# Rotary half swap in the sliding attention layer by transfers inside SBUF in place of a permutation matmul

## The chip, the cores and the metric

The kernel runs on one core of one Trainium2 chip. The metric is the device time of one launch in microseconds (us). A core has a matrix engine (PE, TensorE), a vector engine (DVE), an activation engine (ACT), a general engine (POOL, GpSimd) and a sync engine (SP), each with an instruction stream of its own, and 16 DMA engines that move data between HBM and the on-chip memory SBUF, or inside SBUF. PSUM is the memory into which PE writes. Engines wait for one another through semaphores only. An engine runs its instructions in the order of its program: one that waits holds up all behind it.

## The reference

One inference step of a small encoder: 256 prompt frames and 32 sample frames, model width 1024. Layer 0 mixes by an mLSTM, layer 1 by sliding-window attention with 16 query heads, 4 key and value heads and width 64. Each mixer has half a SwiGLU feed-forward before and behind it. What the change touches is the rotary embedding of layer 1's queries and keys:

```python
def rope(x, pos):
    inv = ROPE_THETA ** (-jnp.arange(0, A_HD, 2, dtype=jnp.float32) / A_HD)
    ang = pos.astype(jnp.float32)[:, None] * inv[None, :]
    cos = jnp.cos(ang)[None, :, None, :]
    sin = jnp.sin(ang)[None, :, None, :]
    xf = x.astype(jnp.float32)
    x1, x2 = xf[..., : A_HD // 2], xf[..., A_HD // 2:]
    return jnp.concatenate([x1 * cos - x2 * sin, x2 * cos + x1 * sin], axis=-1).astype(x.dtype)

def swa_project(x, w_qkv, pos):
    ...
    q, k, v = jnp.split(x @ w_qkv, [A_HEADS * A_HD, (A_HEADS + A_KV_HEADS) * A_HD], axis=-1)
    q = rope(q.reshape(B, T, A_HEADS, A_HD), pos)
    k = rope(k.reshape(B, T, A_KV_HEADS, A_HD), pos)
```

Then come the scores with a mask and a sink, the softmax, the product with the values, and the output projection.

## The kernel before

Activations are kept with features on partitions: x is 8 chunks of 128 features by 288 tokens. Every weight product is made to nearly fp32 from three matmuls of rounded parts (hi*hi, hi*lo, lo*hi; `products`, L360 to L362), so one **piece** (128 output features, 8 input chunks) is 24 matmuls of 288 columns on PE. The weights stream from HBM: SP issues one transfer of 1 MB for two pieces (L303) into one of two `raw` buffers, ACT rounds a piece to `whi` (L340, `split_hi`), DVE subtracts to get `wlo` (L347, `split_lo`), and PE multiplies. SP may load unit u when both pieces of unit u-2 have been subtracted (`lo_done`, L322).

The program is twelve stages, one behind the other. Stage 8, `swa_in`, makes the 12 pieces of the attention layer in the order of `SWA_PIECES`: k0, q0, v0, q1, q2, q3, k1, q4, q5, q6, v1, q7. Numbers 0 to 11 of this list are called **steps** below, step n being what an engine does around piece n. `lo_ahead` in step n subtracts the weights of piece n+4; step 1 does it for pieces 4 and 5.

Rotary: DVE copies a q or k piece out of PSUM to `s_raw` (L1201). PE multiplies it by a permutation matrix `perm`, which exchanges the 32-partition halves of each head (L642, an fp32 product of 288 columns into a PSUM bank of the ring `acc`). DVE multiplies the result by sin into `s_t2` (L1219). POOL makes the product with cos (`s_t1`, L1332) and the sum (L1336), which is the rotated piece. `ROPE` is the list of the ten pieces that are not v.

The attention itself is cut into 20 items (16 of prompt, 4 of sample) that run as a pipeline of **ticks** between the pieces: from step 4 on there are two ticks in a step. In tick t PE makes scores of items t and t+1 if t is even (L578, L580, L585), transposes the probabilities of item t-2 (L595 to L598), and multiplies by the values (L614, L621, L625); DVE takes mask and row maximum of item t's scores (L1149, L1152, `scores`) and divides item t-1 (L1163 to L1167, `divide`); ACT does the exponentials (L867), copies out the transposed probabilities (L852) and the results (L842). Scores of item t on PE need the rotated q (`rope_done`) and the maximum of item t-1 (`neg_ready`). v pieces are transposed on PE (L646, "turn") and copied by DVE (L1223, L1224).

The order of the groups of PE and DVE around this is the list `SWA_GROUPS`, 24 entries: 12 pieces, 10 swaps, each behind the next piece, and 2 turns. The ticks hang on entries of this list (`SWA_TICKS`). Ticks 16 to 23 (`TAIL_TICKS`) follow step 11 and are mixed with parts of stage 9, `mix_out`.

Of the kernel before, what the change touches and what calls it, by code (L numbers as in the profile page):

```python
# [43 lines left out]
          ("swa_in", 6, 24, 8), ("mix_out", 4, 8, 8), ("ffn_in", 22, 44, 8), ("ffn_out", 8, 8, 11)]  # L44
# [15 lines left out]
for _n, _p in enumerate(SWA_PIECES):  # L60
    SWA_GROUPS.append(("piece", _p))
    if _n and SWA_PIECES[_n - 1] in ROPE:
        SWA_GROUPS.append(("swap", SWA_PIECES[_n - 1]))
    if _p in TURN_AFTER:
        SWA_GROUPS.append(("turn", TURN_AFTER[_p]))
SWA_GROUPS.append(("swap", SWA_PIECES[-1]))
# [8 lines left out]
SWA_TICKS = {}  # L75
for _n in range(FIRST_TICK, len(SWA_PIECES)):
    _g = SWA_GROUPS.index(("piece", SWA_PIECES[_n]))
    SWA_TICKS[SWA_GROUPS[_g]], SWA_TICKS[SWA_GROUPS[_g + 1]] = 2 * (_n - FIRST_TICK), 2 * (_n - FIRST_TICK) + 1
TAIL_TICKS = range(2 * (len(SWA_PIECES) - FIRST_TICK), len(ITEMS) + 4)

# [16 lines left out]
C_ID, C_ONE, C_PERM, C_TRI, C_SEL = 0, 128, 256, 384, 640  # L97
# [7 lines left out]
def constants():  # L105
# [5 lines left out]
    c[p, C_PERM + (p ^ 32)] = 1.0  # L111
# [18 lines left out]
def program(nc, a):  # L130

    ctx = ExitStack()
    with ctx:
# [21 lines left out]
        cst = sb("cst", [P, 3 * P])  # L155
# [9 lines left out]
        ident, ones, perm = cst[:, 0:P], cst[:, P:2 * P], cst[:, 2 * P:3 * P]  # L165
# [35 lines left out]
        s_qs = w(9920, 2, 4 * TS)  # L201

# [70 lines left out]
        t1_ready = sem("t1_ready")  # L273
        rope_done = sem("rope_done")
# [24 lines left out]
        def _(sp):  # L299
# [75 lines left out]
        def _(pe):  # L375
# [17 lines left out]
            def in_piece(i, it, c, g, G):  # L393
# [4 lines left out]
                products(pe, group_bank(g), c % 4, [(k, k) for k in range(KD)], xhi, xlo, True, True).then_inc(piece_done, 1)  # L398
# [168 lines left out]
            def tick(t, G0):  # L567
# [32 lines left out]
                if t >= 4 and t % 2 == 0:  # L600
# [3 lines left out]
                    pe.wait_ge(evac, G0 + group_of("turn", f"v{c // 4 if kind == 'p' else c}") + 1)  # L604
# [23 lines left out]
            def swa_in(i):  # L628
                c0_, G0 = 2 * FIRST_UNIT[i], FIRST_GROUP[i]
                pe.wait_ge(mix_in, MIX_SWA)  # L630
                for g, (what, p) in enumerate(SWA_GROUPS):
                    n = SWA_PIECES.index(p)
                    bank = group_bank(g)
                    if what == "piece":
                        if n == 0:
                            first_two(i, c0_, G0)
                        if n > 1:
                            in_piece(i, 0, c0_ + n, g, G0 + g)
                    elif what == "swap":
# [3 lines left out]
                    else:  # L643
                        pe.wait_ge(evac, max(G0 + group_of("piece", p) + 1, G0 + g - 3))
                        for t, (at, m) in enumerate(TOK):
                            mm = pe.transpose(acc[(g + BANK) % 4][0:m, t * P:(t + 1) * P], s_vT[:, at:at + m], ident)  # L646
                        mm.then_inc(turn_mm, 1)
                    if (what, p) in SWA_TICKS:
                        tick(SWA_TICKS[what, p], G0)

# [35 lines left out]
        def _(act):  # L686
# [183 lines left out]
            def swa_in(i, norm):  # L870
# [4 lines left out]
                for what, p in SWA_GROUPS:  # L875
                    if what == "piece":
                        hi_ahead(0, c0_ + SWA_PIECES.index(p))
                    if (what, p) in SWA_TICKS:
                        tick(SWA_TICKS[what, p])
# [7 lines left out]
            for m in range(KD):  # L887
                if m == 4:
                    act.dma_start(cst[:, :], a["cst"][:, 0:3 * P]).then_inc(cst_in, 16)
# [40 lines left out]
        def _(dve):  # L930
# [257 lines left out]
            def swa_in(i, norm):  # L1188
                c0_ = 2 * FIRST_UNIT[i]
                for g, (what, p) in enumerate(SWA_GROUPS):  # L1190
                    n = SWA_PIECES.index(p)
                    bank = group_bank(g)
                    xi = ROPE.index(p) if p in ROPE else None
                    if what == "piece":
                        dve.wait_ge(piece_done, c0_ + n + 1)
                        if xi is None:
                            dve.tensor_tensor(s_vT[:, :], bank, rstd[:, :], ALU.mult).then_inc(evac, 1)
                        else:
                            if xi >= 2:
                                dve.wait_ge(t1_ready, xi - 1)  # L1200
                            dve.tensor_copy(s_raw[:, xi % 2, :], bank).then_inc(evac, 1)  # L1201
                        if n == 1:
# [4 lines left out]
                            own(dve.tensor_tensor(rs, sin, rstd[:, :], ALU.mult))  # L1207
                        if n >= FIRST_TICK:
                            divide(2 * (n - FIRST_TICK))
                        if n == 1:  # L1210
                            lo_ahead(0, c0_)
                        if n > 0:
                            lo_ahead(0, c0_ + n)
                    else:
                        dve.wait_ge(turn_mm, TURNS.index((what, p)) + 1)
                        if what == "swap":
                            if xi >= 2:
                                dve.wait_ge(rope_done, xi - 1)
                            dve.tensor_tensor(s_t2[:, xi % 2, :], bank, rs, ALU.mult).then_inc(evac, 1)  # L1219
                        else:  # L1220
                            j = int(p[1]) * P
                            bank = acc[(g + BANK) % 4]
                            dve.tensor_copy(s_v[0:TS, 2, j:j + P], bank[0:TS, 2 * P:3 * P])  # L1223
                            dve.tensor_copy(s_v[:, 0:2, j:j + P], bank[:, 0:2 * P].rearrange("p (t c) -> p t c", t=2))\  # L1224
                                .then_inc(evac, 1)
                    if (what, p) in SWA_TICKS:
# [219 lines left out]
```

## Time and profile before

| what | us |
|---|---|
| time, median of 3 runs | 1119.02 |
| lowest and highest run | 1117.14, 1119.58 |
| span of the profiled execution (first to last instruction) | 1116.9 |
| PE busy | 1099.2 (98%) |
| DVE busy | 707.9 (63%) |
| ACT busy | 510.8 (46%) |
| POOL busy | 126.0 (11%) |

The profiled execution has no time of its own in the records beside its span of 1116.9 us; the span is 2.1 us under the median of the runs. "Busy" is an average over all twelve stages; the attention stage (about 802 to 875 us) has other shares than the rest, so it is read from windows of its own. In a row of the trace a start is in us from the span's start, and L642 is line 642 of the kernel.

### The profile page before, as it was taken

The numbers are of one execution on the slowest core, as the hardware profiler recorded it, in microseconds if no ns is written. First come the engines' busy times: TensorE is split into PE (matmuls) and PEld (weight loads), VectorE is DVE, ScalarE is ACT, GpSimd is POOL, SyncE is SP. The second block draws the span as 40 slices with busy tenths as digits, with TensorE's granted clock in tenths as the row PEclk, the third lists the DMA queues.
The fourth block names the chain that finished last, engine by engine and source line by source line (L and its number), as shares of the span: only waits on it lengthen the run. The fifth ranks groups of instructions, "written<-read, shape, count | busy, mean of one in ns | idle before, by whom it ended". The sixth has DMA issues, their size and how long they took to land.

```text
span 1116.9 us, 21215 instructions
## 1 busy us (share of the span) xinstructions
PE 1099.2 (98%) x8113; PEld 1075.8 (96%) x8113; DVE 707.9 (63%) x1073; ACT 510.8 (46%) x760; POOL 126.0 (11%) x159
## 2 busy tenths in 40 slices
PE   8999999999999999999999999999999999999996
PEld 7999999998999999999999999999988899999996
DVE  7766665564665866666546666645599776666442
ACT  6444443354454544444335444433466554444331
POOL 3000001100002600000120000011142410000011
PEclk9999999999999999999999999999999999999998
DMA  6544454432332654445434544543332244444531
GB/s 235 188 172 166 153 204 156 151 107 102 127 123 89 216 188 150 172 180 184 179 113 154 182 153 156 204 176 141 113 142 97 82 172 162 173 165 178 182 129 43
DMA packets 24203, 172.04 MB, mean 154 GB/s; under 512 B 3248, under 2 KB 3536, under 8 KB 5600
## 3 DMA queue, kind: packets, MB, share of 16 engines
q1 hardware_dynamic: 21888, 167.16, 41.6%
q0 software_dynamic: 960, 2.23, 0.6%
q10 hardware_dynamic: 1312, 2.07, 0.5%
q8 instruction: 29, 0.48, 0.2%
q14 instruction: 14, 0.11, 0.0%
HBM read 168.88 MB, written 2.56 MB: 153 GB/s over the span
## 4 chain that ended last, share of the span: by engine, by line
PE 93%; DVE 3%; ACT 2%; DMA 1%; issue 1%; POOL 0%; DVEq 0%; ACTq 0%; SPq 0%
PE acc L360 30%; PE acc L362 29%; PE acc L361 29%; DVE wlo L347 1%; DMA raw<-in_w 1%; DVE rstd L946 1%; PE mb L595 0%; ACT whi L340 0%; PE mb L614 0%; PE mb L529 0%; PE num L521 0%; PE acc L642 0%; ACT work L867 0%; PE mb L387 0%; PE num L524 0%
## 5 line engine op out<-in xcount | busy, mean ns | idle before, releaser
L360 PE MATMUL acc<-xhi,whi 128*128 128x288 f32 x1696 | 508.1, 300 | 3.3 <-DVE xlo L941 2.8
L340 ACT ACTIVATE whi<-raw 128x1024 fp32r<-128x1024 f32 (+1 forms) x292 | 328.8, 1128 | 390.1 <-PE acc L362 373.7
L361 PE MATMUL acc<-xlo,whi 128*128 128x288 f32 x1696 | 502.3, 296 | 0.0
L362 PE MATMUL acc<-xhi,wlo 128*128 128x288 f32 x1696 | 500.5, 295 | 0.0
L347 DVE TENSOR_TENSOR wlo<-raw,whi 128x1024 fp32r<-128x1024 f32 (+1 forms) x292 | 389.2, 1333 | 158.7 <-ACT whi L340 148.7
L360 PEld LDWEIGHTS acc<-xhi,whi 128*128 128x128 f32 x1696 | 319.6, 188 | 7.2 <-issue 4.5
L362 PEld LDWEIGHTS acc<-xhi,wlo 128*128 128x128 f32 x1696 | 321.3, 189 | 0.0
L361 PEld LDWEIGHTS acc<-xlo,whi 128*128 128x128 f32 x1696 | 320.4, 189 | 0.5
L360 PE MATMUL acc<-ahi,whi 128*128 128x288 f32 x832 | 247.1, 297 | 0.9 <-DVE alo L1179 0.7
L361 PE MATMUL acc<-alo,whi 128*128 128x288 f32 x832 | 245.4, 295 | 0.0
L362 PE MATMUL acc<-ahi,wlo 128*128 128x288 f32 x832 | 244.6, 294 | 0.0
L360 PEld LDWEIGHTS acc<-ahi,whi 128*128 128x128 f32 x832 | 155.9, 187 | 2.2 <-issue 1.2
L362 PEld LDWEIGHTS acc<-ahi,wlo 128*128 128x128 f32 x832 | 156.7, 188 | 0.0
L361 PEld LDWEIGHTS acc<-alo,whi 128*128 128x128 f32 x832 | 156.2, 188 | 0.0
L968 DVE TENSOR_TENSOR work<-acc,rstd 128x288 f32<-128x288 f32 x88 | 40.2, 456 | 59.5 <-PE acc L362 58.7
L1280 POOL TENSOR_TENSOR ssq<-x 128x288 f32<-128x288 f32 x7 | 4.7, 665 | 612.3 <-DVE x L995 582.9
L1291 POOL TENSOR_TENSOR sqr<-x 128x288 f32<-128x288 f32 x44 | 42.6, 969 | 201.9 <-DVE x L995 197.8
L964 DVE TENSOR_TENSOR work<-acc,rstd 128x288 f32<-128x288 f32 x88 | 40.2, 456 | 34.8 <-PE acc L362 34.6
L745 ACT ACTIVATE xhi<-x,norms (+1 forms) x24 | 12.9, 537 | 92.4 <-DVE x L995 92.4
L995 DVE SCALAR_TENSOR_TENSOR x<-acc,x 128x288 f32 (+1 forms) x32 | 14.6, 458 | 61.2 <-PE acc L362 61.2
L971 DVE TENSOR_TENSOR work<-work 128x288 f32<-128x288 f32 x88 | 40.3, 458 | 6.9 <-DVE work L968 2.2
L719 ACT ACTIVATE ahi<-work 128x288 f32 (+1 forms) x88 | 39.0, 443 | 10.8 <-DVE work L971 8.7
(208 smaller groups left out, 618.4 us busy)
## 6 DMA issues: line engine op xcount, KB each, us to landing
raw<-in_w SPq DMA_DIRECT2D x113, 1024.0 KB, 4.8
raw<-in_w SPq DMA_DIRECT2D x32, 1408.0 KB, 5.8
x<-in_xT SPq DMA_DIRECT2D x4, 288.0 KB, 5.8
raw<-in_w SPq DMA_DIRECT2D x2, 512.0 KB, 5.2
out_yT<-x ACTq DMA_DIRECT2D x3, 288.0 KB, 2.3
work<-in_cst POOLq DMA_DIRECT2D x1, 560.0 KB, 4.0
work<-in_c ACTq DMA_DIRECT2D x1, 514.0 KB
out_cp<-work POOLq DMA_DIRECT2D x4, 128.5 KB, 2.4
```

The source lines that it names most:

```text
L340: act.activation(dst, src, ACT.Copy).then_inc(hi_done, 1)
L347: dve.tensor_tensor(dst, src, hi, ALU.subtract).then_inc(lo_done, 1)
L360: pe.matmul(out, wh, hi[:, k, :], start=(first and n == 0), stop=False)
L361: pe.matmul(out, wh, lo[:, k, :], start=False, stop=False)
L362: mm = pe.matmul(out, wl, hi[:, k, :], start=False, stop=(last and n == len(tiles) - 1))
L719: act.activation(ahi[:, bass.ds(2 * it + u, 1), :], f_prod[:, u % 2:u % 2 + 1, :], ACT.Copy)\
L745: act.activation(xhi[:, m, :] if norm < N_FINAL else xg[:, m, :], x[:, m, :], ACT.Copy, scale=norms[:, norm, m]).then_inc(xhi_done, 1)
L964: dve.tensor_tensor(f_gate[:, b, :], group_bank(2 * u), rstd[:, :], ALU.mult).then_inc(evac, 1)
L968: dve.tensor_tensor(f_up[:, b, :], group_bank(2 * u + 1), rstd[:, :], ALU.mult).then_inc(evac, 1)
L971: dve.tensor_tensor(f_prod[:, b, :], f_silu[:, b, :], f_up[:, b, :], ALU.mult).then_inc(prod_done, 1)
L995: dve.scalar_tensor_tensor(x[:, m, :], acc[u][:, 0:T].rearrange("p (a t) -> p a t", a=1), 0.5, x[:, m, :], ALU.mult, ALU.add).then_inc(eva ...
L1291: pool.tensor_tensor(sqr[:, m % 2, :], x[:, m, :], x[:, m, :], ALU.mult).then_inc(pool_sq, 1)
```

## The change

The permutation matmul and its matrix are dropped. A piece's half swap is made by four transfers inside SBUF, of 32 partitions each, from `s_raw` to a new buffer `s_swap`, issued by SP (`halves_swapped`); SP's loads for stages 8 and 9 are written out by hand so that the swaps can stand among them. DVE's product with sin reads `s_swap` (`swapped`), directly behind the `lo_ahead` of the next step and ahead of both ticks. `SWA_GROUPS` has 16 entries: 12 pieces, 2 turns, and 2 "last" (the third transpose of a turn, now a group of its own). On PE the odd tick stands in the middle of a piece (`between`).

```diff
-STAGES: ("swa_in", 6, 24, 8)
+STAGES: ("swa_in", 6, 16, 8)
...
+            def swa_load(u):
+                i, m = (8, u) if u < STAGES[8][1] else (9, u - STAGES[8][1])
+                sp.wait_ge(lo_done, 2 * (FIRST_UNIT[8] + u - 2) + 2)
+                load(a[f"w{i}"][m], 8, 0, FIRST_UNIT[8] + u)
+
+            def halves_swapped(xi, p):
+                b = xi % 2
+                sp.wait_ge(evac, FIRST_GROUP[8] + group_of("piece", p) + 1)
+                if xi >= 2:
+                    sp.wait_ge(t2_ready, xi - 1)
+                for at in range(0, P, 32):
+                    sp.dma_start(s_swap[at:at + 32, b, :], s_raw[at ^ 32:(at ^ 32) + 32, b, :]).then_inc(swap_in[b], 16)
...
+                if i == 8:
+                    for u in range(4):
+                        swa_load(u)
+                    for n, p in enumerate(SWA_PIECES):
+                        if n % 2 == 0:
+                            swa_load(4 + n // 2)
+                        if p in ROPE:
+                            halves_swapped(ROPE.index(p), p)
+                if i in (8, 9):
+                    continue
...
 PE, swa_in
-                        pe.wait_ge(evac, max(G0 + group_of("piece", p) + 1, G0 + g - 3))
-                        pe.matmul(bank, perm, s_raw[:, ROPE.index(p) % 2, :], start=True, stop=True).then_inc(turn_mm, 1)
...
+                            t = 2 * (n - FIRST_TICK) - 1
+                            in_piece(i, 0, c0_ + n, g, G0 + g, between=(lambda: tick(t, G0)) if t > 0 else None)
+                        if p in SWA_TICKS:
+                            tick(SWA_TICKS[p], G0)
...
 DVE, swa_in
+                def swapped(xi):
+                    b = xi % 2
+                    dve.wait_ge(swap_in[b], SWAP * (xi // 2 + 1))
+                    if xi >= 2:
+                        dve.wait_ge(rope_done, xi - 1)
+                    dve.tensor_tensor(s_t2[:, b, :], s_swap[:, b, :], rs, ALU.mult).then_inc(t2_ready, 1)
...
                         if n > 0:
                             lo_ahead(0, c0_ + n)
+                        if n and SWA_PIECES[n - 1] in ROPE:
+                            swapped(ROPE.index(SWA_PIECES[n - 1]))
+                        if p in SWA_TICKS:
+                            tick(SWA_TICKS[p])
+                            tick(SWA_TICKS[p] + 1)
...
-                            dve.tensor_tensor(s_t2[:, xi % 2, :], bank, rs, ALU.mult).then_inc(evac, 1)
...
+                swapped(len(ROPE) - 1)
                 for t in TAIL_TICKS:
...
 POOL
-                pool.wait_ge(evac, G0 + group_of("swap", p) + 1)
+                pool.wait_ge(t2_ready, xi + 1)
```

SP's queue in stages 8 and 9. Before, it holds loads only (`w8` and `w9` are the weights of stages 8 and 9; each waits for `lo_done`):

```order
L303 ISA [waits lo_done]
L303 DMA raw<-in_w8 128x2048
L322 REGISTER_ALU
L303 ISA [waits lo_done]
L303 DMA raw<-in_w8 128x2048
```

Now, from the first load of stage 8 (units 0 to 4) to the swaps of steps 4 and 5:

```order
L302 DMA raw<-in_w8 128x2048 [waits lo_done] x5
L324 DMA work<-work 32x288 [waits evac]
L324 DMA work<-work 32x288 x3
L324 DMA work<-work 32x288 [waits evac]
L324 DMA work<-work 32x288 x3
L302 DMA raw<-in_w8 128x2048 [waits lo_done]
L324 DMA work<-work 32x288 [waits t2_ready,evac]
L324 DMA work<-work 32x288 x3
L302 DMA raw<-in_w9 128x2048 [waits lo_done]
L324 DMA work<-work 32x288 [waits t2_ready,evac]
L324 DMA work<-work 32x288 x3
L324 DMA work<-work 32x288 [waits t2_ready,evac]
```

The swap of an even step stands behind a load that waits for `lo_done`; the swap of the odd step behind it follows at once.

DVE in steps 1 to 3, before (L347 is the subtraction, L1219 the product with sin, L1197 and L1201 the evacuations of a piece):

```order
L347 TENSOR_TENSOR wlo<-raw,whi 128x1024 [waits hi_done,vector_chain]
L347 TENSOR_TENSOR wlo<-raw,whi 128x1024 [waits hi_done]
L1219 TENSOR_TENSOR work<-acc0,work 128x288 [waits turn_mm]
L1197 TENSOR_TENSOR work<-acc1,rstd 128x288 [waits piece_done]
L347 TENSOR_TENSOR wlo<-raw,whi 128x1024 [waits hi_done]
L1219 TENSOR_TENSOR work<-acc2,work 128x288 [waits turn_mm]
L1201 COPY work<-acc3 128x288 [waits t1_ready,piece_done]
```

And now (L370, L1225, L1233, L1238 are the same operations):

```order
L370 TENSOR_TENSOR wlo<-raw,whi 128x1024 [waits hi_done,vector_chain]
L370 TENSOR_TENSOR wlo<-raw,whi 128x1024 [waits hi_done]
L1225 TENSOR_TENSOR work<-work 128x288 [waits swap_in0]
L1233 TENSOR_TENSOR work<-acc0,rstd 128x288 [waits piece_done]
L370 TENSOR_TENSOR wlo<-raw,whi 128x1024 [waits hi_done]
L1225 TENSOR_TENSOR work<-work 128x288 [waits swap_in1]
L1238 COPY work<-acc1 128x288 [waits t1_ready,piece_done]
```

The wait of the product with sin has moved from a matmul of PE (`turn_mm`) to the landing of the transfers (`swap_in0`, `swap_in1`); its place behind the subtractions is the same here. From step 5 on it stands ahead of both ticks' maxima in place of between them:

```order
L370 TENSOR_TENSOR wlo<-raw,whi 128x1024 [waits hi_done]
L1225 TENSOR_TENSOR work<-work 128x288 [waits rope_done,swap_in1]
L1177 ISA work<-num,work 128x128 [waits s_mm]
L1177 ISA work 128x1
L1177 ISA work<-num,work 128x256
```

## Rows read from the trace of the kernel before

**Rows 1.** The page: span and busy time of the engines.

```profile
span 1116.9 us, 21215 instructions
...
PE 1099.2 (98%) x8113; PEld 1075.8 (96%) x8113; DVE 707.9 (63%) x1073; ACT 510.8 (46%) x760; POOL 126.0 (11%) x159
```

**Rows 2.** Window: length, busy PE, PEld, DVE, ACT, POOL, granted clock, DMA share, GB/s.

```profile
815.00:860.00 45.00, 44.60 (x354) 37.46 (x355) 42.77 (x155) 28.39 (x95) 12.51 (x21) 1.00 0.25 93
```

**Rows 3.** Chain in order of time, one step of PE: start us, us, what.

```profile
824.79 0.42 PE num L578 x4
825.21 0.43 PE num L580 x4
...
826.95 0.68 PE acc L642 x2
...
831.15 0.42 PE num L578 x4
```

**Rows 4.** Timeline of DVE, step 6: start, us, line, tiles.

```profile
825.46 0.45 DVE L1201 COPY work<-acc 128x288 f32<-128x288 f32 x1
...
828.62 0.45 DVE L1219 TENSOR_TENSOR work<-acc,work 128x288 f32<-128x288 f32 x1
...
831.60 0.44 DVE L1201 COPY work<-acc 128x288 f32<-128x288 f32 x1
```

**Rows 5.** Timeline of DVE, subtractions and marks of steps 1 to 5.

```profile
806.20 2.85 DVE L347 TENSOR_TENSOR wlo<-raw,whi 128x1024 fp32r<-128x1024 f32 x2
...
812.04 1.26 DVE L347 TENSOR_TENSOR wlo<-raw,whi 128x1024 fp32r<-128x1024 f32 x1
...
816.23 0.28 DVE L1149 CUSTOM_DVE_ANT_0 work<-num,work 128x128 f32<-128x128 f32 x1
...
820.88 1.22 DVE L347 TENSOR_TENSOR wlo<-raw,whi 128x1024 fp32r<-128x1024 f32 x1
```

**Rows 6.** Timeline of SP: starts of loads 4 and 6 of stage 8.

```profile
809.22 0.33 SPq L303 DMA_DIRECT2D raw<-in_w  x1
...
822.27 0.33 SPq L303 DMA_DIRECT2D raw<-in_w  x1
```

**Rows 7.** Issues: tiles, queue, count, KB, median us to landing; load 4, then the page.

```profile
raw<-in_w SPq DMA_DIRECT2D x1, 1024.0 KB, 4.8
...
out_yT<-x SPq DMA_DIRECT2D x1, 288.0 KB, 2.3
```

**Rows 8.** Timeline of SP at the program's start, transfers issued behind one another.

```profile
2.14 0.43 SPq L311 DMA_DIRECT2D raw<-in_w  x1
2.62 1.02 SPq L312 DMA_DIRECT2D x<-in_xT  x2
```

**Rows 9.** Issues of those two starts, alone: KB, us to landing.

```profile
raw<-in_w SPq DMA_DIRECT2D x1, 512.0 KB, 6.1
...
x<-in_xT SPq DMA_DIRECT2D x1, 288.0 KB, 6.4
```

**Rows 10.** Timeline of POOL: sum and product with cos; DVE's division beside it, then alone.

```profile
829.15 0.81 POOL L1336 TENSOR_TENSOR work<-work 128x288 f32<-128x288 f32 x1 [3.95 <-DVE work L1219]
...
830.19 0.81 POOL L1332 TENSOR_TENSOR work<-work 128x288 f32<-128x288 f32 x1
...
830.35 0.99 DVE L1167 TENSOR_SCALAR work<-work 128x128 f32<-128x128 f32 x2
...
832.34 0.55 DVE L1167 TENSOR_SCALAR work<-work 128x128 f32<-128x128 f32 x2
```

**Rows 11.** Timeline of DVE: subtraction of step 11 and maximum of tick 16.

```profile
857.79 1.21 DVE L347 TENSOR_TENSOR wlo<-raw,whi 128x1024 fp32r<-128x1024 f32 x1
...
863.62 0.28 DVE L1149 CUSTOM_DVE_ANT_0 work<-num,work 128x128 f32<-128x128 f32 x1
```

**Rows 12.** Windows at the span's end, columns as in rows 2.

```profile
1108.00:1110.00 2.00, 0.00 (x0) 0.00 (x0) 1.48 (x1) 0.49 (x1) 0.00 (x0) 0.96 0.01 4
1110.00:1112.00 2.00, 0.00 (x0) 0.00 (x0) 1.97 (x4) 0.00 (x0) 1.45 (x2) 0.50 0.00 0
```

More of the change, by code:

```diff
@@ L59 @@
 SWA_GROUPS = []
-for _n, _p in enumerate(SWA_PIECES):
+for _p in SWA_PIECES:
     SWA_GROUPS.append(("piece", _p))
-    if _n and SWA_PIECES[_n - 1] in ROPE:
-        SWA_GROUPS.append(("swap", SWA_PIECES[_n - 1]))
     if _p in TURN_AFTER:
-        SWA_GROUPS.append(("turn", TURN_AFTER[_p]))
-SWA_GROUPS.append(("swap", SWA_PIECES[-1]))
+        SWA_GROUPS += [("turn", TURN_AFTER[_p]), ("last", TURN_AFTER[_p])]
 TURNS = [g for g in SWA_GROUPS if g[0] != "piece"]
@@ L74 @@
 FIRST_TICK = 4
[L75 to L78, printed above, removed]
+SWA_TICKS = {_p: 2 * (_n - FIRST_TICK) for _n, _p in enumerate(SWA_PIECES) if _n >= FIRST_TICK}
 TAIL_TICKS = range(2 * (len(SWA_PIECES) - FIRST_TICK), len(ITEMS) + 4)
+SWAP = 64
 FILL = {}
@@ L94 @@
 N_F1, N_FINAL, N_HEAD = 0, 6, 7
[L97 removed]
+C_ID, C_ONE, C_TRI, C_SEL = 0, 128, 256, 512
 C_COS = C_SEL + NH * P
@@ L164, in program @@
         work = sb("work", [P, 12496])
-        ident, ones, perm = cst[:, 0:P], cst[:, P:2 * P], cst[:, 2 * P:3 * P]
+        ident, ones = cst[:, 0:P], cst[:, P:2 * P]
         def w(at, *shape):
@@ L391, in ss_sum, with in_piece @@
                 mm.then_inc(ss_mm, 1)
-            def in_piece(i, it, c, g, G):
+            def in_piece(i, it, c, g, G, between=None):
                 pe.wait_ge(lo_done, 4 * it + c + 1)
@@ L397, in in_piece @@
                     pe.wait_ge(evac, 4 * it + G - 3)
-                products(pe, group_bank(g), c % 4, [(k, k) for k in range(KD)], xhi, xlo, True, True).then_inc(piece_done, 1)
+                if between is None:
+                    products(pe, group_bank(g), c % 4, [(k, k) for k in range(KD)], xhi, xlo, True, True).then_inc(piece_done, 1)
+                    return
+                products(pe, group_bank(g), c % 4, [(k, k) for k in range(KD // 2)], xhi, xlo, True, False)
+                between()
+                products(pe, group_bank(g), c % 4, [(k, k) for k in range(KD // 2, KD)], xhi, xlo, False, True)\
+                    .then_inc(piece_done, 1)
             def first_two(i, c, G):
@@ L603, in tick @@
                     pe.wait_ge(pt_ready, t - 2)
-                    pe.wait_ge(evac, G0 + group_of("turn", f"v{c // 4 if kind == 'p' else c}") + 1)
+                    pe.wait_ge(evac, G0 + group_of("last", f"v{c // 4 if kind == 'p' else c}") + 1)
                     if t >= 6:
@@ L637, in swa_in @@
                         if n > 1:
[L638 to L645 removed]
+                            t = 2 * (n - FIRST_TICK) - 1
+                            in_piece(i, 0, c0_ + n, g, G0 + g, between=(lambda: tick(t, G0)) if t > 0 else None)
+                        if p in SWA_TICKS:
+                            tick(SWA_TICKS[p], G0)
+                        continue
+                    pe.wait_ge(evac, max(G0 + group_of("piece", p) + 1, G0 + g - 3))
+                    for t, (at, m) in enumerate(TOK):
+                        if (t == 2) == (what == "last"):
                             mm = pe.transpose(acc[(g + BANK) % 4][0:m, t * P:(t + 1) * P], s_vT[:, at:at + m], ident)
[L647 to L649 removed]
+                    mm.then_inc(turn_mm, 1)
+                tick(TAIL_TICKS[0] - 1, G0)
             def swa_out(i):
@@ L874, in swa_in @@
                 act.activation(warm[:, 9:10], epst[:, :], ACT.Exp)
[L875 to L879, printed above, removed]
+                for n, p in enumerate(SWA_PIECES):
+                    hi_ahead(0, c0_ + n)
+                    if p in SWA_TICKS:
+                        tick(SWA_TICKS[p])
+                        tick(SWA_TICKS[p] + 1)
                 for t in TAIL_TICKS:
@@ L1341, in _ @@
             pool.dma_start(a["kT_out"], s_k[:, :, TP - P:T]).then_inc(out_dma, 16)
-            pool.wait_ge(evac, G0 + group_of("turn", "v1") + 1)
+            pool.wait_ge(evac, G0 + group_of("last", "v1") + 1)
             pool.dma_start(a["v_out"][0:P, :], s_v[:, 1, :]).then_inc(out_dma, 16)
```

35 lines of the change are left out of this document (17 added, 18 removed).

## The prediction

> **What bounds the kernel now.** The page comes first: of a span of 1116.9 us PE is busy for 1099.2 and DVE for 707.9 [rows 1]. Over the whole program PE is the bound, and work taken from PE looks like time won. But the change lies in one stage, so the second view is the window of that stage alone: from 815 to 860 us, steps 4 to 11, PE is busy for 44.60 of 45.00 us and DVE for 42.77, which is 95% [rows 2]. There are two bounds here, and the less loaded one is hardly idle. The third view is the stage in order of time. On PE one step repeats from 824.79 to 831.15, 6.36 us, and holds one permutation of 0.68 us [rows 3]. On DVE the same step runs from one evacuation at 825.46 to the next at 831.60, 6.14 us [rows 4]. The fourth view is SP's queue, which the change puts to a new use: load 4 starts at 809.22, when the two subtractions of step 1 end (806.20 + 2.85 = 809.05), and load 6 at 822.27, when that of step 5 ends (820.88 + 1.22 = 822.10) [rows 5, 6]. So in an odd step n SP's load starts 0.17 us behind DVE's `lo_ahead(n)`; by the code this holds for steps 1, 3, 5, 7, 9 and 11.
>
> **What is removed.** Ten permutations of 0.68 us [rows 3], 6.8 us of PE. The most that this can bring is 6.8 us, if PE alone set the end. It does not: with 0.68 taken away PE's step is 5.68 us and DVE's stays 6.14, since DVE's own work is the same list of operations (the product with sin only reads SBUF in place of PSUM; no row prices that form, and I leave it at the 0.45 us of L1219 [rows 4], some 0.4 from start to start). Even with a free swap a step falls from 6.36 to 6.14 only. The matrix's smaller constant load and the eight groups fewer in `SWA_GROUPS` cost nothing and win nothing: the banks of PSUM are freed by the evacuations as before. The odd tick in the middle of a piece keeps PE supplied while it waits for a transpose's input; PE will not be the bound, so I put it at nothing.
>
> **What is added, and where it waits.** Forty transfers of 36 KB. Their place in SP's queue decides. Take step 5. DVE ends `lo_ahead(5)` and then, as its next instruction, wants the swapped q2. SP meanwhile holds load 6 at the head of its queue, which waits for exactly that `lo_ahead(5)`; q2's four transfers are queued behind it. So although q2 was in `s_raw` a whole step earlier, its swap is only issued when DVE is already asking for it, and the whole flight of the transfer is a wait of DVE. The same meets k0 in step 1, k1 in step 7 and q5 in step 9. The swaps of the odd pieces (q0, q3, q4, q6) follow directly behind the even ones and are asked for a step later, so they are hidden. q1 and q7 are odd pieces that stand behind a load of their own (v0 and v1 need no swap), and are counted apart below.
>
> **The price of one such wait, W.** From the end of `lo_ahead(n)`: 0.17 us until the load starts, then the load's own flight of 4.8 us [rows 7], if transfers of one queue are served in their order, then the swaps' own share. The program's start shows the order: a 512 KB transfer issued at 2.14 lands 6.1 later, at 8.24; one of 288 KB issued right behind it at 2.62 lands 6.4 later, at 9.02 [rows 8, 9]. The later one lands later, by 0.8 us for 288 KB. Four swaps are 144 KB, so half of that, 0.4. W = 0.17 + 4.8 + 0.4 = 5.4 us. Lower end: the swaps pass the load. Then SP's issues count: the load's 0.33, three swaps of about 0.5 before the last [rows 6, 8], and a flight of 2.3 us, which is the 288 KB output alone on its queue [rows 7]: 0.17 + 0.33 + 1.5 + 2.3 = 4.3. Upper end: each transfer touches 32 partitions where the 288 KB one touches 128; if it is four times as slow for that, 1.6 in place of 0.4: W = 6.6. I take 5.4, since its rows show this very queue in this very situation.
>
> A rule of the notes bears on W. The Trainium skill, DMA: Bandwidth & Descriptors, section "Anatomy of one DMA", gives about 2.0 us of fixed cost for each transfer plus its bytes at 436 GB/s. By it load and swaps together (1.2 MB) would take an estimated 4.7 us, W would be 4.9, and the time some 3 us less than by the rows. The section "Queues, rings and completion order" of the same page has descriptors taken up in ring order, and with that the landings of rows 8 and 9 agree.
>
> **What is queued behind the wait.** On DVE: both ticks' row maxima and the division, then the next evacuation. ACT's exponentials wait for the maxima, and PE's next scores (even tick) wait for `neg_ready` from them. PE can still do its even tick, the next piece and the odd tick's transposes, and then stands. Nothing on DVE can be drawn ahead, so W is paid in full.
>
> **The sum,** as the shift of DVE's work against its times of before.
> - Step 1: k0's swap arrives at 809.05 + 5.4 = 814.45. Then two products with sin, two evacuations (0.4 each) and two subtractions (1.2 each [rows 5]), 4.0 in all: `lo_ahead(3)` ends at 818.45. Before it ended at 812.04 + 1.26 = 813.30 [rows 5].
> - Step 4: load 5 starts then, and q1's swap lands 5.4 later, at 823.85. The turn's copies, q2's evacuation and `lo_ahead(4)` fill 2.2 of it. First maximum at 824.25, before 816.23 [rows 5]: +8.0, and +7.6 at the start of step 5, as the product with sin is already done.
> - Steps 5, 7, 9: 3 x 5.4 = +16.2, in all +23.8.
> - Back: DVE's division takes 0.99 us while POOL runs L1332 beside it, and 0.55 alone [rows 10]. Now POOL's sum and product start 0.8 us earlier in the tick and are mostly over by then: 8 odd ticks x 0.44 = 3.5 at most. DVE's few idle gaps (45.00 - 42.77 = 2.2) are partly filled too. I take 3.0: +20.8.
> - Tail: q7's swap is issued behind load 9, which waits for `lo_ahead(11)`. From the end of that subtraction (859.00 [rows 11]) the first maximum of tick 16 comes after W 5.4, the product 0.4, POOL's start and sum 0.15 + 0.81 [rows 10], PE's start and scores 0.1 + 0.85 [rows 3]: 7.7. Before it came at 863.62, 4.6 later [rows 11]. +3.1: +23.9.
> - PE's clock. In each of the long waits PE stands: of a pair of steps of some 17 us it has 2 x 5.68 = 11.4 us of work, so about 5.5 us in one piece. The trace shows what a stop does: with no matmul after 1108 the granted clock is 0.96 from 1108 to 1110 and 0.50, 1.2 in place of 2.4 GHz, from 1110 on [rows 12]. So part of the work behind each stop runs at half rate. Most of it lies under DVE; not so in the tail, where tick by tick PE is in the chain. Below 0 this cannot be. Above: PE takes up work again when W's end is 2.0 us past (product and two maxima), and has a whole step, 5.7, before the next piece is finished, at 7.7; DVE asks for that piece at 3.7 + 6.1 = 9.8. At half rate the step costs 5.7 more, of which 2.1 fit there: 3.6 a pair, 11 for three. I take 2, nearer to nothing, because the stops are short against the work between them and DVE has the later work. +26.
>
> The Trainium skill, TensorE: Matmul & The Clock Gate, section "What's actually happening", says the same of an idle array (1.2 GHz when cold, 2.4 when busy); rows 12 agree.
>
> 1119.0 + 26 = **1145 us**. The sum was made on the profiled execution, whose span is 2.1 us under the median; the shift is added to the median.
>
> **The rivals.**
> (a) The swap is hidden, the kernel is faster. That holds if a swap lands before DVE asks, by an SP that isn't held behind `lo_done`, or a landing within a fraction of a us. Then steps 5 to 11 gain 0.2 each, the two permutations ahead of step 4 bring 1.4: about 3 us, 1116. Against it stand rows 5 and 6 and the order of SP's queue. Chance 4%.
> (b) The swaps pass the load. W = 4.3: six waits (steps 1, 4, 5, 7, 9, tail) of 1.1 less, and no clock lost: 23.9 - 6.6 = 17, 1136. For it: nothing shows how transfers inside SBUF stand to one from HBM. Chance 18%.
> (c) Slow 32-partition transfers, or the half clock in the path: W = 6.6 adds 6 x 1.2 = 7, the clock takes 11 in place of 2: 23.9 + 7 + 11 = 42, 1161. Decided by how much of PE's work behind a stop runs at 1.2 GHz. Chance 20% for the half of this way and beyond.
> (d) The change doesn't do what it says, because the wait only takes the place of one that was there: then the time is within 0.2% of before, which is about what a measurement of this kernel can tell from no change. DVE at 95% speaks against it. 1%.
>
> **How the numbers follow.** Forecast 57%, 1139 to 1151, time 1145. (b) 18%, (c) 20%, (a) 4%, (d) 1%. The range 1135 to 1160 takes in (b) and (c) and leaves out (a), (d) and the edges. Faster by over 0.2%: 4%. Within: 1%. Slower: 95%.
>
> **What the profile of the changed kernel would show.** DVE idle ahead of the product with sin, released by the swap's transfer, in steps 1, 4, 5, 7, 9 and behind tick 15, about 5 us in four of them, and next to none in steps 2, 6, 8 and 10. SP's swaps of even steps starting right behind a load, and landing behind it. The window of steps 4 to 11 about 20 us longer, PE's busy share in it down to some 70%, with dips of the granted clock. Division at 0.55 in place of 0.99. All other stages alike. I would be wrong if DVE's waits are near 2 us or absent (then the queue isn't served as I say), or if the waits are there and the span is longer by much less (then DVE wasn't the bound), or by much more (then PE at half rate is).

## The result, and the profile after

The changed kernel takes 1161.1 us (median) against 1119.3 before: a ratio of 1.0367, with a 95% interval of 1.0343 to 1.0392. The forecast was 1145, in a range of 1135 to 1160. It is slower, as forecast, by the mechanism that was forecast, but by 42 us and not by 26, and the time lies a little outside the range. Of its four executions one took 3743.66 us, stands apart as slow and is left out of the ratio; the other three lie between 1156.25 and 1161.21.

The page of the changed kernel, answering to rows 1:

```profile
span 1159.3 us, 21181 instructions
...
PE 1110.0 (96%) x8093; PEld 1085.3 (94%) x8093; DVE 707.6 (61%) x1073; ACT 510.9 (44%) x760; POOL 126.1 (11%) x159
```

DVE's busy time has not changed (707.9 before), though the span is 42.4 us longer. PE has twenty instructions fewer (the ten permutations, each of two passes) and is busy for 10.8 us more: part of its work ran slower.

Windows of the attention stage (length, busy PE, PEld, DVE, ACT, POOL, granted clock, DMA share, GB/s). Before, 815 to 860 us was 99% PE and 95% DVE at a clock of 1.00 [rows 2]. After:

```profile
815.00:835.00 20.00, 13.01 (x82) 11.81 (x83) 11.85 (x31) 4.62 (x13) 7.18 (x9) 0.83 0.32 115
835.00:855.00 20.00, 13.22 (x98) 10.84 (x97) 11.84 (x44) 8.49 (x27) 3.54 (x6) 0.83 0.22 68
855.00:875.00 20.00, 14.74 (x105) 12.55 (x103) 10.82 (x38) 7.74 (x25) 3.52 (x6) 0.83 0.23 72
875.00:895.00 20.00, 14.74 (x99) 11.96 (x97) 12.98 (x51) 8.56 (x29) 3.57 (x6) 0.74 0.18 64
```

DVE is idle for 35 to 46% of each window and PE for 26 to 35%. Step 5 shows where the idle time comes from. The timelines of DVE and SP (L370 is the subtraction, L1225 the product with sin; L302 loads, L324 swaps; in brackets the idle time ahead of an instruction and what ended it):

```profile
834.14 1.22 DVE L370 TENSOR_TENSOR wlo<-raw,whi 128x1024 fp32r<-128x1024 f32 x1
841.46 0.46 DVE L1225 TENSOR_TENSOR work<-work 128x288 f32<-128x288 f32 x1 [6.10 <-DMA work<-work]
...
835.38 0.33 SPq L302 DMA_DIRECT2D raw<-in_w  x1
835.82 4.94 SPq L324 DMA_DIRECT2D work<-work  x8
```

The subtraction ends at 835.36, SP's load starts at 835.38, q2's four swaps from 835.82, and DVE stands for 6.10 us. SP's order is what was read from its queue; each issue of a swap takes 0.6 us. Who DVE and PE waited for in the whole stage (us in total, times, longest):

```profile
DVE work L1225 <- DMA work<-work: 28.4, 6, 6.1
DVE work L1238 <- PE acc L385: 7.4, 5, 2.7
DVE work L1191 <- ACT work L896: 6.0, 12, 2.6
...
PE num L607 <- DVE work L1180: 14.1, 3, 6.8
PE acc L675 <- DVE work L1233: 6.9, 1, 6.9
PE num L607 <- POOL work L1373: 6.2, 1, 6.2
```

Exactly six waits for the swaps, as counted: 6.1 us in steps 1, 5, 7 and 9 (6.11, 6.10, 5.95, 6.04), 1.4 in step 4, 2.8 in the tail.

To compare kernels, the stage is measured from the start of load 3 on SP to the first output of stage 9 on DVE. Before, from 799.44, 77.45 us; after, 116.32:

```profile
799.44 0.33 SPq L303 DMA_DIRECT2D raw<-in_w  x1
...
876.89 0.46 DVE L1014 TENSOR_TENSOR x<-acc,x 128x288 f32<-128x288 f32 x1 [1.95 <-PE acc L362]
```

```profile
803.00 10.11 SPq L302 DMA_DIRECT2D raw<-in_w  x2
...
919.32 0.46 DVE L1042 TENSOR_TENSOR x<-acc,x 128x288 f32<-128x288 f32 x1 [1.95 <-PE acc L385]
```

That is 38.9 us. The other 3.5 us of the two spans' difference lie ahead of the stage, in the mLSTM stage, which the change does not touch. There PE's clock falls for some us in nearly every kernel, for a length that differs; the profile of the changed kernel caught a long one. The same window of before and of after:

```profile
245.00:270.00 25.00, 24.85 (x150) 21.57 (x149) 16.68 (x42) 11.75 (x27) 0.00 (x0) 0.93 0.37 126
```

```profile
245.00:270.00 25.00, 24.85 (x134) 21.88 (x133) 15.60 (x42) 11.16 (x25) 0.00 (x0) 0.80 0.28 91
```

PE does not stop there. In the changed kernel the fall comes while it works on products of four rows, with no gap above 0.15 us; the window from 251 to 253 is at 0.53, where 0.50 is 1.2 GHz:

```profile
249.16 1.21 PE L514 MATMUL mb<-work 4*128 4x288 f32 x4
250.22 0.64 PE L514 MATMUL num<-work 4*128 4x288 f32 x2
251.01 1.24 PE L514 MATMUL num<-work 4*128 4x288 f32 x2 [0.15 <-DVE acol L1072]
```

```profile
251.00:253.00 2.00, 1.99 (x5) 1.23 (x6) 2.00 (x10) 1.38 (x5) 0.00 (x0) 0.53 0.94 393
```

In the kernel before, the clock stays at 1.00 behind the same products and falls behind the next group of four rows, some 6 us later; in e6 below it stays at 1.00 behind both.

In the profiles of the other kernels this stage's clock in the window from 245 to 270 lies between 0.80 and 1.00, and load 3 starts between 796.15 and 803.00, the later the lower that clock, with up to 2 us between kernels of the same clock. So a total time below carries some 3 us of chance from a stage that is the same everywhere, and the length of the attention stage is the sharper measure.

### The profile page after: what moved, and what is told of

It is laid out like the page before. It is cut to its first block, busy times and chain, and to the rows that moved or that the text cites. A ratio compares the mean times of both kernels' runs of the same rounds, so it can differ in the third digit from the quotient of the medians.

```text
span 1159.3 us, 21181 instructions
## 1 busy us (share of the span) xinstructions
PE 1110.0 (96%) x8093; PEld 1085.3 (94%) x8093; DVE 707.6 (61%) x1073; ACT 510.9 (44%) x760; POOL 126.1 (11%) x159
## 4 chain that ended last, share of the span: by engine, by line
PE 90%; DVE 4%; DMA 2%; ACT 1%; SPq 1%; issue 1%; DVEq 0%; POOL 0%; ACTq 0%
PE acc L383 29%; PE acc L384 28%; PE acc L385 28%; DMA work<-work 2%; DVE wlo L370 1%; SPq L324 1%; PE mb L643 1%; PE mb L624 1%; DVE rstd L974 1%; DMA raw<-in_w 0%; ACT whi L363 0%; PE mb L558 0%; PE num L550 0%; DVE work L1177 0%; PE num L609 0%
## 5 line engine op out<-in xcount | busy, mean ns | idle before, releaser
L370 DVE TENSOR_TENSOR wlo<-raw,whi 128x1024 fp32r<-128x1024 f32 (+1 forms) x292 | 388.9, 1332 | 161.2 <-ACT whi L363 151.3
L383 PEld LDWEIGHTS acc<-xhi,whi 128*128 128x128 f32 x1696 | 323.2, 191 | 8.8 <-issue 6.5
L385 PEld LDWEIGHTS acc<-xhi,wlo 128*128 128x128 f32 x1696 | 325.0, 192 | 0.0
L384 PEld LDWEIGHTS acc<-xlo,whi 128*128 128x128 f32 x1696 | 324.1, 191 | 0.3
L773 ACT ACTIVATE xhi<-x,norms (+1 forms) x24 | 12.9, 537 | 92.4 <-DVE x L1023 92.4
```

The costliest lines, as they stand in the source:

```text
L370: dve.tensor_tensor(dst, src, hi, ALU.subtract).then_inc(lo_done, 1)
L383: pe.matmul(out, wh, hi[:, k, :], start=(first and n == 0), stop=False)
L384: pe.matmul(out, wh, lo[:, k, :], start=False, stop=False)
L385: mm = pe.matmul(out, wl, hi[:, k, :], start=False, stop=(last and n == len(tiles) - 1))
L773: act.activation(xhi[:, m, :] if norm < N_FINAL else xg[:, m, :], x[:, m, :], ACT.Copy, scale=norms[:, norm, m]).then_inc(xhi_done, 1)
```

## The experiments

All kernels on one table. "q7" is the time from load 3 to the evacuation of q7, the "tail" the rest of the stage; both from the one profiled execution.

| kernel | time, us | ratio to before (95%) | stage | q7 | tail |
|---|---|---|---|---|---|
| before | 1118.7 to 1119.3 | 1 | 77.45 | 56.74 | 20.71 |
| changed | 1161.1 | 1.0367 (1.0343, 1.0392) | 116.32 | 88.50 | 27.82 |
| e1 swap first | 1123.2 | 1.0030 (1.0015, 1.0045) | 81.86 | 57.45 | 24.41 |
| e2 load behind | 1146.3 | 1.0235 (1.0209, 1.0261) | 105.67 | 78.22 | 27.45 |
| e3 PE busy in steps | 1156.3 | 1.0329 (1.0304, 1.0355) | 115.61 | 87.54 | 28.07 |
| e4 no transfers | 1123.4 | 1.0042 (1.0025, 1.0059) | 81.86 | 57.46 | 24.40 |
| e5 q7's product early | 1121.9 | 1.0026 (1.0010, 1.0041) | 79.24 | 57.43 | 21.81 |
| e6 products between ticks | 1119.4 | 1.0012 (0.9997, 1.0027) | 79.76 | 55.89 | 23.87 |
| e7 one transfer | 1155.0 | 1.0334 (1.0311, 1.0357) | 114.68 | 87.19 | 27.49 |
| e8 PE busy in steps and tail | 1153.5 | 1.0302 (1.0275, 1.0329) | 111.82 | 85.96 | 25.86 |
| e9 before, no permutation | 1117.7 | 0.9996 (0.9985, 1.0007) | 76.42 | 55.76 | 20.66 |
| e10 q7 by permutation | 1117.7 | 0.9990 (0.9975, 1.0004) | 76.54 | 55.86 | 20.68 |

**Theory and rival.** The theory was that the loss is the place of the swaps in SP's queue, behind a load that itself waits for DVE. The rival was that the transfers are slow or disturb the stage wherever they stand.

### e1: the swaps ahead of the load

```diff
                     for n, p in enumerate(SWA_PIECES):
-                        if n % 2 == 0:
-                            swa_load(4 + n // 2)
                         if p in ROPE:
                             halves_swapped(ROPE.index(p), p)
+                        if n % 2 == 1:
+                            swa_load(4 + n // 2)
```

> The changed kernel with SP's queue in another order: the swaps of an even and an odd step stand ahead of the load that waits for lo_ahead, not behind it; nothing else differs. Theory (the swaps are late only because they queue behind a load that waits for DVE): a swap is issued when its piece is evacuated, lands some 4.5 us later, before DVE asks for it; the six waits of 28.4 us in all are gone, and the time is 1113 to 1119. Rival (transfers inside SBUF of 32 partitions are slow or disturb the stage wherever they stand): waits of over 3 us remain and the time stays over 1135.

The stage falls from 116.32 to 81.86 us, and DVE no longer waits for a single swap. The rival is refuted: the forty transfers as such cost the stage nothing. But the time is 1123.2, above the 1119 expected and clearly above before. The theory holds for 34.5 of the 38.9 us; 4.4 are something else.

### e4: no transfers at all

```diff
...
-                    dve.wait_ge(swap_in[b], SWAP * (xi // 2 + 1))
+                    dve.wait_ge(evac, FIRST_GROUP[8] + group_of("piece", ROPE[xi]) + 1)
...
-                    dve.tensor_tensor(s_t2[:, b, :], s_swap[:, b, :], rs, ALU.mult).then_inc(t2_ready, 1)
+                    dve.tensor_tensor(s_t2[:, b, :], s_raw[:, b, :], rs, ALU.mult).then_inc(t2_ready, 1)
```

SP issues loads only, so the product reads the unswapped piece.

> The changed kernel without the 40 transfers; the product with sin reads the unswapped piece, so the rotary embedding is wrong and the time is that of a swap that costs nothing. Theory (DVE is the second bound of the stage): not the 6.8 us of the permutations but about 3 come back, 1115 to 1117. Rival (PE was the only bound): 1112.

Both expectations miss: with a swap that costs nothing the new order is slower than before, 1.0042, with a stage of 81.86 us, equal to e1's. So the 4.4 us are not the transfers' either. Its profile names two causes. First, PE stands for q7. Who PE waited for:

```profile
PE num L604 <- POOL work L1371: 4.3, 2, 3.7
```

q7's product stands behind both last ticks on DVE (`swapped` after the loop), so POOL's sum comes late, PE stands 3.7 us ahead of tick 16, and the granted clock over 855 to 875 is 0.91. Second, DVE's step has not become shorter. The end of step 7 in the kernel before, where the step took 6.13 us (831.60 [rows 4] to 837.73):

```profile
836.09 0.17 DVE L1163 TENSOR_TENSOR work<-work 128x2 f32<-128x2 f32 x1
...
836.49 0.99 DVE L1167 TENSOR_SCALAR work<-work 128x128 f32<-128x128 f32 x2
...
837.73 0.44 DVE L1201 COPY work<-acc 128x288 f32<-128x288 f32 x1
```

And step 7 in e4:

```profile
832.32 0.45 DVE L1236 COPY work<-acc 128x288 f32<-128x288 f32 x1
...
836.45 0.29 DVE L1174 CUSTOM_DVE_ANT_0 work<-num,work 128x128 f32<-128x128 f32 x1 [0.16 <-issue]
...
837.53 0.16 DVE L1188 TENSOR_TENSOR work<-work 128x2 f32<-128x2 f32 x1 [0.17 <-ACT work L893]
...
837.92 0.55 DVE L1192 TENSOR_SCALAR work<-work 128x128 f32<-128x128 f32 x2
...
838.72 0.45 DVE L1236 COPY work<-acc 128x288 f32<-128x288 f32 x1
```

It takes 6.40. The division is down to 0.55 us from 0.99 [rows 10], as forecast. But with the product no longer between the two maxima, DVE waits 0.16 us ahead of the second maximum and 0.17 us for ACT's exponentials ahead of the division, where before it waited for neither, and smaller gaps open between its own dependent instructions.

### e9: the kernel before without permutations

```diff
-                        pe.wait_ge(evac, max(G0 + group_of("piece", p) + 1, G0 + g - 3))
-                        pe.matmul(bank, perm, s_raw[:, ROPE.index(p) % 2, :], start=True, stop=True).then_inc(turn_mm, 1)
...
-                            dve.tensor_tensor(s_t2[:, xi % 2, :], bank, rs, ALU.mult).then_inc(evac, 1)
+                            dve.tensor_tensor(s_t2[:, xi % 2, :], s_raw[:, xi % 2, :], rs, ALU.mult).then_inc(evac, 1)
```

> The kernel before without the ten permutations on PE; the product with sin reads the unswapped piece (the rotary embedding is wrong), all else in the old order. Prices what the change takes away. If DVE is the second bound: 1115 to 1117. If PE alone was the bound: 1112.

The stage shortens by 1.0 us of the 6.8 that the permutations occupy on PE, less than the 2 to 4 expected, and the ratio cannot be told from 1. With DVE's work in this order that is all there was to win: DVE is the second bound, right behind PE.

### e2: the wait kept, the load behind

```diff
-                            swa_load(4 + n // 2)
+                            sp.wait_ge(lo_done, 2 * (FIRST_UNIT[8] + 4 + n // 2 - 2) + 2)
                         if p in ROPE:
                             halves_swapped(ROPE.index(p), p)
+                        if n % 2 == 1:
+                            swa_load(4 + n // 2)
```

> The changed kernel, but only the load is moved behind the swaps of its pair of steps; SP still waits for lo_ahead before the even swap. Tells what of the 6.1 us wait is the load in front. If the load's flight sets the landing: the wait falls to 0.2 + 4 issues of 0.6 + a flight of about 2 us = 4.3 to 4.6, six times 1.5 less, time about 1150. If SP's issues and the swaps' own flight set it: the wait falls by the load's issue of 0.44 only, to 5.7, time about 1158.

The long waits fall from 6.1 to 3.8 us, below even the 4.3 to 4.6 expected for a load that sets the landing. The issues of four swaps, just behind the subtraction, in this kernel and behind a load in the changed one (KB each, us to landing):

```profile
work<-work SPq DMA_DIRECT2D x4, 36.0 KB, 1.9
```

```profile
raw<-in_w SPq DMA_DIRECT2D x1, 1024.0 KB, 5.3
work<-work SPq DMA_DIRECT2D x4, 36.0 KB, 4.3
```

A swap alone lands in 1.9 us, behind a load in 4.3. So of the 6.1 us, 2.3 are the load in front, and 3.8 are a transfer's own flight with three issues ahead of the last. The stage is 10.7 us shorter (six waits of up to 2.3 us less; 9 expected); the time fell by 14.8; in the profiles 3.5 of that lie ahead of the stage, where load 3 starts at 799.54.

### e7: one transfer in place of four

```diff
-SWAP = 64
+SWAP = 16
...
-                for at in range(0, P, 32):
-                    sp.dma_start(s_swap[at:at + 32, b, :], s_raw[at ^ 32:(at ^ 32) + 32, b, :]).then_inc(swap_in[b], 16)
+                sp.dma_start(s_swap[:, b, :], s_raw[:, b, :]).then_inc(swap_in[b], 16)
```

> The changed kernel with one transfer of all 128 partitions for a piece in place of four of 32, in the same place of SP's queue; it swaps nothing, so the rotary embedding is wrong. Tells what of the 6.1 us is four issues of 0.6 us. If SP's issues make the landing late: 0.17 + 0.43 + a flight of 4 to 4.5 = 4.8 to 5.1, time about 1155 (six waits of 1 us less). If the load in front sets it: 5.6 to 6.0, time 1159 to 1161.

It swaps nothing. The longest wait is 5.9 us and the sum of the six 26.8, against 6.1 and 28.4; the stage is 1.6 us shorter. Behind a load the number of issues hardly matters: the queue is what sets the landing. The time of 1155.0 looks like the other answer, but 4.2 us of the difference between the two profiles lie ahead of the stage (load 3 starts at 798.84, in the changed kernel at 803.00); the stage decides.

### e3 and e8: PE kept busy while it waits

`keep_busy` and the fillers of steps 6, 8 and 10 are in both; the 44 at q1, ahead of v0's turn, are in e3 alone, the 40 ahead of tick 16 in e8 alone.

```diff
+            def keep_busy(g, G0, count):
+                pe.wait_ge(evac, G0 + g - 2)
+                for _ in range(count):
+                    pe.matmul(group_bank(g + 1), xhi[:, 0, 0:P], xhi[:, 0, :], start=True, stop=True)
...
+                        if n in (6, 8, 10):
+                            keep_busy(g, G0, 40)
...
+                        if p == "q1":
+                            keep_busy(g, G0, 44)
...
+                    if t == TAIL_TICKS[0]:
+                        pe.wait_ge(evac, FIRST_GROUP[i])
+                        for _ in range(40):
+                            pe.matmul(group_bank(3), xhi[:, 0, 0:P], xhi[:, 0, :], start=True, stop=True)
```

> The changed kernel with matmuls of no use in PE's stops: 40 before the even tick of steps 6, 8 and 10 and 44 before the turn of v0 (about 5.3 and 5.9 us), written to the next free bank. DVE's waits for the swaps stay at 6 us. Theory (the rest of the miss is work at 1.2 GHz behind the stops): the granted clock stays 1.00 there, DVE's waits for PE (1.3 us in steps 9 and 11, 1.75 in step 4) vanish, time 1148 to 1154. Rival (DVE's waits alone make the loss, the clock is covered): 1159 to 1162, or later if the fillers overrun the stops.

> The changed kernel with 40 matmuls of no use ahead of the even tick of steps 6, 8 and 10, as in the run before with fillers, but none at v0's turn and 40 ahead of tick 16, where PE stands 6 us for q7. Tells how much of the tail's loss (from q7's evacuation to the first output of the next stage 27.8 us, 20.7 before) is work at 1.2 GHz. If the clock is the larger part of what the wait for q7 doesn't explain: the tail falls to 25.5 or less. If it is covered: 27.5 to 28.5.

First the rows on the clock in the changed kernel. PE stops at about 837 in step 5 and takes up work at 843.9:

```profile
835.00:840.00 5.00, 2.11 (x17) 1.88 (x15) 0.36 (x1) 0.00 (x0) 0.00 (x0) 1.00 0.71 228
840.00:845.00 5.00, 1.11 (x8) 0.94 (x8) 3.19 (x16) 2.15 (x9) 1.75 (x3) 0.66 0.13 41
845.00:850.00 5.00, 5.00 (x33) 3.86 (x30) 4.71 (x17) 2.92 (x10) 1.78 (x3) 0.65 0.02 3
```

The granted clock falls during the stop and stays down for some us after it (0.65, a mean of the levels 0.50 and 1.00). With the fillers DVE's waits for late pieces in steps 9 and 11 go (1.30 and 1.27 us in the changed kernel, at most 0.55 in e3). But e3's stage is only 0.7 us shorter, and its time of 1156.3 meets neither expectation. Its fillers at v0's turn brought DVE 2 us earlier to q1's swap in step 4. That won nothing, since this swap is issued behind the subtraction of step 3, whatever PE does; the wait grew from 1.4 to 4.7 us, by those 2 us and by 1.4 that the swap landed later behind load 5. I have no row that says why it landed later. e8, without those and with fillers in the tail, is the cleaner one: 2.5 us less until q7 (85.96 against 88.50) and 2.0 less in the tail (25.86 against 27.82). So 4.5 us of the stage's length are won back by keeping PE busy. It is a net figure and not the whole price of the clock: in e8 the granted clock is still 0.50 from 815 to 820, behind the stop that has no fillers, 0.73 from 840 to 845 and 0.68 from 880 to 885, and the wait of step 9 is 6.9 us in place of 6.0. The 4.5 us are less than the 7 to 13 expected of e3, and in the tail just short of the mark set for e8 (25.5 or less for the clock as the larger part, 27.5 or more for a covered clock).

### e5, e6, e10: towards a version that loses nothing

e5 is e1 with q7's product ahead of tick 15's division. e6 also puts every product back between the two maxima of a step (shown without the branch for the other steps and the old call that goes):

```diff
...
                             tick(SWA_TICKS[p])
+                            if product:
+                                swapped(ROPE.index(SWA_PIECES[n - 1]))
+                            if p == SWA_PIECES[-1]:
+                                scores(SWA_TICKS[p] + 1)
+                                swapped(len(ROPE) - 1)
+                                divide(SWA_TICKS[p] + 1)
+                                outputs_lo(SWA_TICKS[p] + 1)
```

> The kernel with the swaps ahead of the load, and q7's product with sin ahead of tick 15's division in place of behind it. The run with free swaps left PE standing 3.7 us for POOL's sum of q7 ahead of tick 16, with the granted clock down behind it. Theory (that late product is what makes both of those runs slower than before): PE's wait falls under 1 us, the tail shortens by about 3.5, time 1118 to 1120. Rival (the tail is bound by ACT and DVE anyway): still 1122 to 1124.

> As the last, and each step's product with sin back between the maxima of its two ticks, where it stands in the kernel before. With the free swap a step took 6.40 us against 6.14 before, and DVE waited 0.2 us for ACT's exponentials in each. Theory (the product between the maxima was cover for ACT): those waits vanish, steps of 6.1, time 1.5 to 2 us under the last, 1116 to 1118. Rival (the order on DVE is indifferent): equal to the last within 0.5.

e5's tail is 21.81 us, 2.6 shorter than e1's; PE still stands 2.6 us for q7, so "under 1 us" was wrong, and the time of 1121.9 lies between the theory's range and the rival's. e6's steps are down by 1.5 us, to 55.89 for q7: the product between the maxima was indeed cover for ACT. But its tail is 2.1 longer than e5's, so the stage did not gain, and the 1116 to 1118 expected was missed. e6's median is 2.5 us below e5's all the same; the fastest executions of the two are 0.2 us apart (1117.60 and 1117.77), and in the profiles load 3 starts 3.9 us earlier in e6, so this is most likely the chance ahead of the stage. Why the tail is longer, on DVE, on PE and in the windows behind it:

```profile
857.60 0.46 DVE L1225 TENSOR_TENSOR work<-work 128x288 f32<-128x288 f32 x1 [1.14 <-DMA work<-work]
...
859.07 0.80 PE L607 MATMUL num<-work 64*128 64x128 f32 x4 [3.18 <-POOL work L1381]
```

```profile
857.00:859.00 2.00, 0.00 (x0) 0.00 (x0) 1.33 (x5) 1.55 (x7) 0.80 (x2) 0.99 0.78 217
859.00:861.00 2.00, 1.93 (x10) 1.31 (x11) 1.66 (x10) 0.00 (x0) 2.00 (x4) 0.50 0.95 379
861.00:863.00 2.00, 2.00 (x17) 1.50 (x16) 1.38 (x10) 1.41 (x6) 0.08 (x1) 0.66 0.28 96
```

q7 is the last piece: no step follows that would hide its transfer. DVE asks for it 1.1 us too early, PE stands 3.2 us, and its next work, which here is the chain itself, runs at 1.2 GHz. In e5 PE stood for 2.6 us and the clock stayed at 1.00 in every window behind it.

e10 is e6 with the old permutation matmul for q7 alone, into q7's own, already evacuated bank.

> The kernel with swaps ahead of the load and products between ticks, but the last piece q7 is swapped by the permutation matmul, since no later step hides a transfer for it. Theory (the only loss left in that kernel is q7's flight of 5 us and the clock that falls while PE stands for it): the tail is 20.7 us as before, the steps keep their 0.85 us of gain, stage 76.6, time 1117.5 to 1118.5, within the uncertainty of before. Rival (something else in the new order lengthens the tail): stage 78 or more.

The stage is 76.54 us, as expected (76.6), with the tail back at 20.68. Nine of ten swaps are hidden transfers in it. The time, 1117.7, is a ratio of 0.9990 with an interval that holds 1: the 0.9 us which the stage's profile shows are within the uncertainty, and about what e9 gives as the limit.

## Why the prediction was right or wrong

**Right: the bound.** Reading the stage's own windows in place of the page gave that DVE at 95% follows close behind PE. e9 confirms it: 6.8 us taken from PE bring 1.0. For a free swap the forecast's rival (a) said 3.

**Right: the place.** The six waits are where SP's queue says they are, and next to none in the even steps. e1 shows that the order of the queue is the whole cause of them.

**Wrong in size: W.** Forecast 5.4, measured 6.1. Its terms were 0.17 + 4.8 + 0.4. The load itself lands later with swaps behind it (5.3 in place of 4.8 [rows 7]), and the swaps a little more. e2 and e7 show which row was the right one: the queue in order, not SP's issues (whose 0.6 us in place of 0.5 were under-sized as well). That is 0.7 us in step 1, 0.7 in step 4, 1.9 over steps 5, 7 and 9, and 0.7 in the tail, 4.0 in all. Step 4 is easily missed, since DVE's wait there is only 1.4 us; but q1's swap, too, lands 6.1 us behind the subtraction in front of it (823.40 to 829.47), and DVE must have it before the first maximum:

```profile
821.94 1.46 DVE L370 TENSOR_TENSOR wlo<-raw,whi 128x1024 fp32r<-128x1024 f32 x1
...
829.47 0.46 DVE L1225 TENSOR_TENSOR work<-work 128x288 f32<-128x288 f32 x1 [1.42 <-DMA work<-work]
```

The work between the two flights was put at 4.0 us and took 4.5 (818.86 to 823.40). The forecast gave both subtractions 1.2 us; that of step 2 takes 1.67, and 1.68 in the kernel before.

**Wrong in sign: "Back", -3.0.** I took the division's shorter time and DVE's idle gaps as time won. The division did fall to 0.55, but what I moved with it had been cover: the product stood between two maxima while ACT worked. e4 has it alone: steps until q7 0.7 us longer, not 3 shorter. This is the failing step of the prediction: the only term with the wrong sign, where the others were too small. It was argued from one operation's duration, without asking what ran during the operation that moved.

**Wrong in size: the tail.** Forecast +3.1 and a part of the clock's 2, measured +7.1, of which W makes 0.7. Of the 7.1 e4, which waits for no transfer, already has 3.7: q7's product had been put behind tick 15 on DVE. I had priced its landing, but not that PE, standing for it, would then go on at 1.2 GHz in the chain. e8 gets 2.0 of it back.

**Wrong in size: the clock.** Forecast 2 of bounds 0 to 11; e8 wins back 4.5. The argument that DVE has the later work holds in the steps for the most part (2.5 us for three pairs, where the bound was 3.6 a pair), not in the tail. In step 4 DVE waits 1.75 us for a piece made at a lower clock, but q1's swap lands later still and covers it.

Against the working, point by point: start of step 5, forecast +7.6, measured +9.7; until q7, +20.8 against +31.8; the stage, about +26 against +38.9. Of the 11.0 us missing at q7, W makes 3.3, "Back" 3.7 (3.0 not won and 0.7 lost, taken over from e4), the clock 2.5 and the work ahead of load 5 0.5: 10.0. The other 1.0 us no run separates. Of the 4.0 missing in the tail W makes 0.7 and the clock 2.0; the other 1.3 stay open. Both together, less the 2 us that the forecast held for the clock in the whole stage, are the stage's miss of 12.9 but for rounding.

The rest of the profiled span's 42.4 us, 3.5, is the clock in the mLSTM stage, which has nothing to do with the change. With a clock there as in the profile before, the time would have been about 1157.6 and inside the range, as that of one execution (1156.25) is. So which side of 1160 the time falls on is chance; the 12.9 us that the stage was mis-forecast by are not.

Rival (b), swaps passing the load, is refuted by the landing times. Rival (c), slow transfers or half clock in the path, came nearest in time (1161). The prediction says that its range takes this rival in, but the range ends at 1160. That its number was hit is luck: its slow 32-partition transfers are refuted by e7, and of the 11 us for the clock e8 finds 4.5; the rest of the miss is mostly "Back" and the late product of q7, which no rival held.

## What to carry to other kernels

A transfer that replaces work of an engine must be issued when its source is ready. If it shares a queue with loads, look at what the entry in front of it waits for: here the queue waited for the very instruction after which the result was wanted, and the whole flight became a stall on the engine nearest to the bound. Before moving an operation to a "better" place, ask what it covers where it stands, and leave the last of a series, which no later step hides, where it is ready soonest: here on PE, for 0.7 us.

## What the runs showed of the hardware

- On SP's queue a 36 KB transfer inside SBUF lands in 1.9 us without a load ahead of it and in 4.3 us behind a load of 1 MB; four of 32 partitions or one of 128 make hardly a difference there (waits of 6.1 and 5.9 us).
- PE's clock fell to 1.2 GHz behind a stop of 3.2 us in e6 and stayed at 2.4 behind one of 2.6 us in e5. Filling the stops with matmuls of no use saved 4.5 us of the stage's length. A stop is not needed: in the mLSTM stage the clock falls to 1.2 GHz behind matmuls of four rows between which PE stood for at most 0.15 us, in the changed kernel at the first such group, in the kernel before at the second, in e3 and e6 at neither.
- What lies ahead of the attention stage differs by up to 7 us from profile to profile (load 3 at 796.15 in one, 803.00 in another), most of it with how long the clock is down in the mLSTM stage, so that small differences are better read from a stage than from the total.
